# Cross-attention over the cached memory: other buffers and another order for the loads, and two transposes moved ahead of the key transposes

## What is computed

```
def mem_attend(h, mk, mv, wq, wo):
    q = (h @ wq).reshape(bsz, t, M_HEADS, M_HEAD_DIM)          # 4 heads of 256
    s = einsum("bthd,bmhd->bhtm", q, mk) * (M_HEAD_DIM ** -0.5)
    p = softmax(s, axis=-1)
    o = einsum("bhtm,bmhd->bthd", p, mv)
    return o.reshape(bsz, t, M_WIDTH) @ wo

# prompt:  mk, mv are computed from mem_prompt, and are outputs too (mem_k_prompt, mem_v_prompt)
# samples: mk, mv = cache_mem_k[l], cache_mem_v[l], each (8, 256, 4, 256) float32
```

## Time and profile before

| | |
|---|---|
| median of three executions | 2195.84 us |
| the profiled execution, its own time | 2198.57 us |
| its span in the trace | 2196.8 us |
| TensorE busy | 2097.8 us, 95% |
| VectorE busy | 992.3 us, 45% |
| ScalarE busy | 762.1 us, 35% |
| GpSimd busy | 195.9 us, 9% |
| DMA over the whole span | 219.94 MB, 100 GB/s |

### The profile page before, as it was taken

The page is one execution under the profiler, slowest core; times in us unless marked ns, Lnnn a source line. Parts: engine busy times, 40 slices in busy tenths (PEclk is TensorE's granted clock), DMA queues, the critical chain, the costliest instruction groups (busy, mean ns, idle before and its releaser), DMA issues.

```text
span 2196.8 us, 30506 instructions
## 1 busy us (share of the span) xinstructions
PE 2097.8 (95%) x12346; PEld 1850.5 (84%) x12346; DVE 992.3 (45%) x1675; ACT 762.1 (35%) x1314; POOL 195.9 (9%) x454
## 2 busy tenths in 40 slices
PE   7999869999989999999999999999989999999997
PEld 6888649898668999999988888779857999999996
DVE  5453463343534444344444547662553444444443
ACT  3222441243523432323323545333542432233232
POOL 2011111000010000000000114210010000000001
PEclk9999887999999999999999999999999999999999
DMA  6223213124552212222221121442482212222221
GB/s 196 94 92 126 107 58 96 58 87 145 210 195 77 77 58 77 77 87 77 78 91 60 58 77 44 149 152 88 163 317 70 77 58 77 77 87 77 77 77 52
DMA packets 111048, 219.94 MB, mean 100 GB/s; under 512 B 6994, under 2 KB 52350, under 8 KB 110844
## 3 DMA queue, kind: packets, MB, share of 16 engines
q1 hardware_dynamic: 89920, 143.80, 19.7%
q0 software_dynamic: 20416, 72.09, 9.3%
q10 hardware_dynamic: 576, 2.10, 0.2%
HBM read 201.03 MB, written 18.24 MB: 100 GB/s over the span
## 4 chain that ended last, share of the span: by engine, by line
PE 89%; DVE 4%; ACT 3%; DMA 3%; issue 1%; POOL 0%; SPq 0%; ACTq 0%; DVEq 0%; POOLq 0%
PE bank L734 14%; PE bank L736 14%; PE bank L735 14%; PE bank L798 7%; PE bank L794 7%; PE bank L796 7%; PE bank L793 5%; PE bank L795 5%; PE bank L797 5%; DMA kcX<-cache_mem_k 2%; PE bank L1008 1%; PE bank L1097 1%; PE bank L757 1%; PE bank L1075 1%; PE bank L996 1%
## 5 line engine op out<-in xcount | busy, mean ns | idle before, releaser
L1876 DVE TENSOR_TENSOR w_lo<-raw,w_hi 128x1024 fp32r<-128x1024 f32 x265 | 319.1, 1221 | 581.3 <-ACT w_hi L1400 576.9
L1400 ACT ACTIVATE w_hi<-raw 128x1024 fp32r<-128x1024 f32 x265 | 274.1, 1052 | 309.7 <-PE bank L736 254.9
L734 PE MATMUL bank<-w_hi,hT_lo 128*128 128x512 f32 x720 | 287.7, 400 | 3.8 <-DVE w_lo L1876 1.8
L794 PE MATMUL bank<-hT_hi,w_lo 128*128 128x384 f32 (+1 forms) x856 | 289.3, 338 | 0.0
L796 PE MATMUL bank<-hT_lo,w_hi 128*128 128x384 f32 (+1 forms) x856 | 289.3, 338 | 0.0
L798 PE MATMUL bank<-hT_hi,w_hi 128*128 128x384 f32 (+1 forms) x856 | 289.3, 338 | 0.0
L736 PE MATMUL bank<-w_hi,hT_hi 128*128 128x512 f32 x720 | 282.4, 392 | 0.0
L735 PE MATMUL bank<-w_lo,hT_hi 128*128 128x512 f32 x720 | 282.4, 392 | 0.0
L793 PE MATMUL bank<-hT_hi,w_lo 128*128 128x256 f32 (+1 forms) x856 | 239.7, 280 | 0.0
L795 PE MATMUL bank<-hT_lo,w_hi 128*128 128x256 f32 (+1 forms) x856 | 239.0, 279 | 0.0
L797 PE MATMUL bank<-hT_hi,w_hi 128*128 128x256 f32 (+1 forms) x856 | 239.0, 279 | 0.0
(11 more groups left out here) (359 smaller groups left out, 3114.8 us busy)
## 6 DMA issues: line engine op xcount, KB each, us to landing
raw<-w_ffn_gate SPq DMA_DIRECT2D x44, 512.0 KB, 4.0
raw<-w_ffn_up SPq DMA_DIRECT2D x44, 512.0 KB, 5.1
raw<-w_ffn_down SPq DMA_DIRECT2D x22, 1024.0 KB, 4.9
kcX<-cache_mem_k POOLq DMA_DIRECT2D x16, 1024.0 KB, 7.0
vcX<-cache_mem_v POOLq DMA_DIRECT2D x16, 1024.0 KB, 8.7
raw<-w_in_even SPq DMA_DIRECT2D x14, 1024.0 KB, 5.3
raw<-w_in_odd SPq DMA_DIRECT2D x12, 1024.0 KB, 5.1
raw<-w_cq SPq DMA_DIRECT2D x8, 1024.0 KB, 7.2
```

The source lines that it names most:

```text
L734: pe.matmul(out, wl, xh, start=first, stop=False)
L794: pe.matmul(ob, wl, hT_hi[:, k, HA:TOK], start=f, stop=False)
L1400: act.activation(w_hi[:, g % W_SLOTS, 0:n], raw[:, q % 2, UNIT * i:UNIT * i + n], ACT.Copy).then_inc(*hi_made.mark(c, u))
L1876: dve.tensor_tensor(w_lo[:, s, 0:n], raw[:, q % 2, UNIT * i:UNIT * i + n], flat(w_hi[:, s, 0:n]), ALU.subtract).then_inc(*lo_made.mark(c, u))
```

## The change

It has three parts. First, memory: `kcX[1]` moves from 53248 (over `mk`) to 28672 (over `mv`), and `kTX[0]` the other way, from 28672 to 53248. Second, GpSimd's stream: the store `o_mv` is issued right behind `o_mk`; k0 follows when the last prompt scores are made; and k1, which now needs `mv` to be free, waits for `crossP` and for `put["mv"]`. v0 and v1 stand behind k1. ScalarE and VectorE no longer wait for `put["mv"]` in step 0. Third, the order inside a step on TensorE: the transposes of `pS` and `oS` come ahead of the 16 key transposes, and ScalarE copies their results ahead of its two key copies. VectorE's order in a step stays. No instruction is added or taken away but the waits.

```diff
--- before.py
+++ after.py
@@ -351,9 +351,9 @@
         mk = at("mk", 53248, [P, 2, D])
         pX = at("pX", 61440, [P, 2, 2, MEM])
         pXT = at("pXT", 0, [P, TP, H, 2, P])
-        kcX = [at("kcX0", 20480, [P, 2, D]), at("kcX1", 53248, [P, 2, D])]
+        kcX = [at(f"kcX{i}", 20480 + 8192 * i, [P, 2, D]) for i in range(2)]
         vcX = [at(f"vcX{i}", 36864 + 8192 * i, [P, 2, D]) for i in range(2)]
-        kTX = [at("kTX0", 28672, [P, 8, MEM]), at("kTX1", 0, [P, 8, MEM])]
+        kTX = [at("kTX0", 53248, [P, 8, MEM]), at("kTX1", 0, [P, 8, MEM])]
         pS = at("pS", 61440, [P, 2, MEM])
         pST = at("pST", 63488, [P, 2, 2, P])
         oS = at("oS", 65536, [P, 2, MEM])
@@ -597,20 +597,23 @@
                 for m in range(2):
                     pool.wait_ge(*act_done.at("mk", l, m, 1))
                 pool.dma_start(io["o_mk"][l].rearrange("(m p) n -> p m n", p=P), mk[:, :, :]).then_inc(*put["mk"].mark(l))
+                for m in range(2):
+                    pool.wait_ge(*act_done.at("mv", l, m, 1))
+                pool.dma_start(io["o_mv"][l].rearrange("(m p) n -> p m n", p=P), mv[:, :, :]).then_inc(*put["mv"].mark(l))
+
+
                 def mem_kv(cache, b):
                     i = b % 2
                     buf, src = (kcX[i], io["cache_mem_k"]) if cache == "k" else (vcX[i], io["cache_mem_v"])
                     pool.dma_start(buf[:, :, :], src[(l * NB + b) * MEM:(l * NB + b + 1) * MEM, :].rearrange("(m p) n -> p m n", p=P)).then_inc(*loads[f"{cache}x{i}"].mark(l, b))
 
-                pool.wait_ge(*aux_full.at("mkT", l, 1, 1))
+
+                pool.wait_ge(*aux_full.at("sX", l, TP - 1, 1))
                 pool.wait_ge(*put["mk"].at(l))
+                mem_kv("k", 0)
+                pool.wait_ge(*pe_done.at("crossP", l))
+                pool.wait_ge(*put["mv"].at(l))
                 mem_kv("k", 1)
-                for m in range(2):
-                    pool.wait_ge(*act_done.at("mv", l, m, 1))
-                pool.dma_start(io["o_mv"][l].rearrange("(m p) n -> p m n", p=P), mv[:, :, :]).then_inc(*put["mv"].mark(l))
-                pool.wait_ge(*aux_full.at("sX", l, TP - 1, 1))
-                mem_kv("k", 0)
-                pool.wait_ge(*lin_full.at(("cv", l, 1), 1))
                 mem_kv("v", 0)
                 mem_kv("v", 1)
                 for b in range(NB):
@@ -1099,6 +1102,21 @@
                 pe_done.after("crossP", l)
 
                 for s in range(NB + 3):
+                    if 2 <= s < NB + 2:
+                        b = s - 2
+                        pe.wait_ge(*dve_done.at("pS", l, b))
+                        out = lin.open(pe, "pST", l, b)
+                        for m in range(2):
+                            ins = pe.transpose(out[:, P * m:P * m + P], pS[:, b % 2, P * m:P * m + P], ident[:, :])
+                        ins.then_inc(*lin_full.mark("pST", l, b))
+                    if s >= 4 and s % 2 == 0:
+
+                        p = s // 2 - 2
+                        pe.wait_ge(*lin_a.at("oXs", l, p))
+                        out = lin.open(pe, "oXT", l, p)
+                        for j in range(2):
+                            ins = pe.transpose(out[:, P * j:P * j + P], oS[:, p % 2, P * j:P * j + P], ident[:, :])
+                        ins.then_inc(*lin_full.mark("oXT", l, p))
                     if s < NB:
                         pe.wait_ge(*loads[f"kx{s % 2}"].at(l, s))
                         for n in range(4):
@@ -1108,21 +1126,6 @@
                                     k = 2 * n + hd
                                     ins = pe.transpose(out[:, MEM * hd + P * m:MEM * hd + P * m + P], kcX[s % 2][:, m, P * k:P * k + P], ident[:, :])
                             ins.then_inc(*aux_full.mark("kTX", l, s, n))
-                    if 2 <= s < NB + 2:
-                        b = s - 2
-                        pe.wait_ge(*dve_done.at("pS", l, b))
-                        out = lin.open(pe, "pST", l, b)
-                        for m in range(2):
-                            ins = pe.transpose(out[:, P * m:P * m + P], pS[:, b % 2, P * m:P * m + P], ident[:, :])
-                        ins.then_inc(*lin_full.mark("pST", l, b))
-                    if s >= 4 and s % 2 == 0:
-
-                        p = s // 2 - 2
-                        pe.wait_ge(*lin_a.at("oXs", l, p))
-                        out = lin.open(pe, "oXT", l, p)
-                        for j in range(2):
-                            ins = pe.transpose(out[:, P * j:P * j + P], oS[:, p % 2, P * j:P * j + P], ident[:, :])
-                        ins.then_inc(*lin_full.mark("oXT", l, p))
                     if 1 <= s <= NB:
                         b = s - 1
                         pe.wait_ge(*act_done.at("kTX", l, b, 2))
@@ -1634,13 +1637,6 @@
                     act.wait_ge(*lin_full.at("oXp", l, k))
                     act.activation(hT_hi[:, k, 0:SEQ], lin.bank("oXp", l, k)[:, :], ACT.Copy).then_inc(*hT_hi_made.mark("oXp", l, k))
                 for s in range(NB + 3):
-                    if s == 0:
-                        act.wait_ge(*put["mv"].at(l))
-                    if s < NB:
-                        for n in (0, 2):
-                            act.wait_ge(*aux_full.at("kTX", l, s, n))
-                            act.activation(kTX[s % 2][:, 2 * n:2 * n + 2, :], aux.bank("kTX", l, s, n)[:, :].rearrange("p (k m) -> p k m", k=2), ACT.Copy).then_inc(*aux_a.mark("kTX", l, s, n))
-                            act_done.after("kTX", l, s, n)
                     if 2 <= s < NB + 2:
                         b = s - 2
                         act.wait_ge(*lin_full.at("pST", l, b))
@@ -1652,6 +1648,11 @@
                         cols = slice(SEQ + 32 * p, SEQ + 32 * p + 32)
                         act.activation(hT_hi[:, :, cols].rearrange("p (h j) q -> p h j q", j=2), lin.bank("oXT", l, p)[:, 0:2 * P].rearrange("p (j h q) -> p h j q", j=2, h=H),
                                        ACT.Copy).then_inc(*act_done.mark("oX", l, p))
+                    if s < NB:
+                        for n in (0, 2):
+                            act.wait_ge(*aux_full.at("kTX", l, s, n))
+                            act.activation(kTX[s % 2][:, 2 * n:2 * n + 2, :], aux.bank("kTX", l, s, n)[:, :].rearrange("p (k m) -> p k m", k=2), ACT.Copy).then_inc(*aux_a.mark("kTX", l, s, n))
+                            act_done.after("kTX", l, s, n)
                     if 1 <= s <= NB:
                         b = s - 1
                         act.wait_ge(*dve_done.at("negXs", l, b))
@@ -2187,8 +2188,6 @@
                     dve.wait_ge(*hT_hi_made.at("oXp", l, k))
                     dve.tensor_tensor(hT_lo[:, k, 0:SEQ], lin.bank("oXp", l, k)[:, :], flat(hT_hi[:, k, 0:SEQ]), ALU.subtract).then_inc(*lin_v.mark("oXp", l, k))
                 for s in range(NB + 3):
-                    if s == 0:
-                        dve.wait_ge(*put["mv"].at(l))
                     if s < NB:
                         for n in (1, 3):
                             dve.wait_ge(*aux_full.at("kTX", l, s, n))
```

More of the change, by code:

```diff
@@ L1101, in rest @@
                 for s in range(NB + 3):
-                    if s < NB:
-                        pe.wait_ge(*loads[f"kx{s % 2}"].at(l, s))
-                        for n in range(4):
-                            out = aux.open(pe, "kTX", l, s, n)
-                            for hd in range(2):
-                                for m in range(2):
-                                    k = 2 * n + hd
-                                    ins = pe.transpose(out[:, MEM * hd + P * m:MEM * hd + P * m + P], kcX[s % 2][:, m, P * k:P * k + P], ident[:, :])
-                            ins.then_inc(*aux_full.mark("kTX", l, s, n))
                     if 2 <= s < NB + 2:
@@ L1125, in rest @@
                         ins.then_inc(*lin_full.mark("oXT", l, p))
+                    if s < NB:
+                        pe.wait_ge(*loads[f"kx{s % 2}"].at(l, s))
+                        for n in range(4):
+                            out = aux.open(pe, "kTX", l, s, n)
+                            for hd in range(2):
+                                for m in range(2):
+                                    k = 2 * n + hd
+                                    ins = pe.transpose(out[:, MEM * hd + P * m:MEM * hd + P * m + P], kcX[s % 2][:, m, P * k:P * k + P], ident[:, :])
+                            ins.then_inc(*aux_full.mark("kTX", l, s, n))
                     if 1 <= s <= NB:
```

## The result

The changed kernel took 2210.36 us, the median of four executions (2209.39 to 2216.25), against 2194.49 for the kernel before, measured beside it. The ratio is 1.0079, with a 95% interval from 1.0054 to 1.0103: slower by 12 to 23 us. (The two medians alone give 1.0072, 15.9 us, which lies inside it.) All fifteen executions of the changed kernel on record took 2206.50 to 2219.41 us, with a median of 2209.82. The profiled execution took 2207.48 us, with a span of 2205.7.

The account below looks back on a forecast made before the run. The prediction took transfers to bound most of the loop, with room only at its edges. Loads and order, 14.7 us, plus the clock, 3.7, made 18.4 us; against 2195.84 that is 2214.2 us, range 2205 to 2224.

Parts of the forecast that it names:

- rival (1): In the loops, the softmax wait hides and only the loads count: 2205.8 us, or 2209 with the clock; chance 0.14.
- What bounds the loop, and that a delay goes straight into the time: Transfers bind most of the loop; TensorE has 89% of the chain, so its delays go straight into the time.
- Part one, the loads: At the loop's start k1, v0 and v1 are issued later, inside the loop: some 5 us per layer.
- Part two, the order: In each loop step, `pS` ahead of the keys exposes the softmax; a step takes at least 5.33 us in the mean.
- The sum of both parts: Late loads and new order together, in the two loops: 7.5 and 7.2 us, 14.7 us in all.
- Part three, edits at nothing: Dropped `mv` waits, k1 moved from 547 us, swapped addresses, ScalarE's earlier copy: nothing, down to -0.3 us a step.
- Part four, the clock: Step 2's key transposes, behind the longest gap, run at half TensorE clock: 1.85 us in each loop, 3.7 us in all.
- (2): Idle DMA time in the loop takes the three added loads: +1 to +2 us per layer, 2199 us; chance 0.05.
- (3): TensorE's clock stays low through the loop: 21 us per layer more, 2254 us; chance 0.06.
- (4): In the loops, scores and values follow the keys' landing sooner and idle queue time closes: -7 us, 2189 us; chance 0.03.
- (5): The change does nothing, because GpSimd's k1, v0 and v1 came no earlier in truth: no difference; chance 0.01.

Follow-up runs that it names:

- e11: The kernel before, unchanged, run again for a second profile: loops of 46.7 and 45.2 us.
- e1: The changed kernel with the order inside a step taken back on TensorE and ScalarE, so late loads only: ratio 1.0032 to the kernel before.
- e2: The kernel before with `pS` and `oS` ahead of the key transposes on TensorE and ScalarE, its loads kept: ratio 1.0018 to the kernel before.
- e8: The changed kernel with 4 thrown-away matmuls of 512 columns in the gap ahead of step 1's key transposes: ratio 1.0078 to the kernel before.
- e5: The kernel before with key transposes last in each step on TensorE, ScalarE and VectorE, GpSimd's order kept: ratio 1.0024 to the kernel before.
- e10: e5 with v(b) issued ahead of k(b+2) in GpSimd's stream: 2189.40 us against 2195.69 for the kernel before, ratio 0.9967.

## Why the prediction was right

The forecast was 2214.2 us with a range of 2205 to 2224; measured were 2210.36. As a difference, 18.4 us were forecast and 15.9 measured beside the kernel before. The time alone proves little: rival (1) with the clock's part came to 2209. What bears the prediction out is the trace. By its steps:

- *What bounds the loop, and that a delay goes straight into the time.* Right in the main: 14.1 us more in the two loops against the mean of two profiles of before (12.6 and 15.6 against each), 15.9 in the medians. That nothing outside the loops would move by more than 2 us didn't hold for single profiles: 10.5 us less ahead of the first loop and 3.7 more between them, where the kernel before itself moved by 7.7 and 2.8 (e11).
- *Part one, the loads.* Step 1's transposes were expected 5.6 us into the loop, behind a gap of 3.7 us; they began 5.8 us into it (588.45 less 582.69), behind gaps of 3.77 and 3.72. k2 was expected 13.7 us into the loop, it landed at 13.3 (596.0 less 582.69). The loads alone were set at 5 us a loop; e1 has 6.1 by the profile and 3.5 by the whole (7 us for two loops).
- *Part two, the order.* The step was set at 5.33 us in the mean and came out at 5.42: the scores follow each other by 5.31 and 5.52 us in turn in layer 1. The wait for line 2203 was set at 1.1 us and was 1.19. Set at 2.5 us a loop in the sum of both parts; e2 gave 2.3 by the profile and 2 by the whole. Counted from the loop's start, the scores of sequence 7 began at 46.8 and 46.1 us, where 45.7 had been worked out without the clock's part. That all loads of steps 5 to 7 come in time failed narrowly in layer 0: k7 was 0.26 us late.
- *The sum of both parts*, 7.5 and 7.2 us for loops of 52.0 us: measured 52.7 and 51.8.
- *Part three, edits at nothing.* Nothing in the trace speaks against it; it wasn't tried apart.
- *Part four, the clock: mis-sized, in the place.* The clock fell in the first gap, between 587 and 588 us, and came back between 594 and 595, as the stretches below show. But the slow blocks were step 1's, not step 2's. They stand in the chain that ended last, and yet cost next to nothing: they and the softmax behind them were over 0.25 us (layer 0) and 0.15 us (layer 1) after k2 had landed, and without them step 2 would have waited for k2. So where 1.85 us a loop had been put down, some 0.2 were paid, and the gap ahead of step 2 (1.98 us) is put down to line 2203 and not to a `kcX` load, as the prediction had it. That the clock's term is too large by 3.3 us and the forecast too high by 3.8 is near enough, but no proof, with medians of the kernel before that differ by 1.4 us. e8 shows the forecast course when step 1 is kept at full clock.
- *Rivals.* (1), the softmax hidden, is refuted by the chain of the changed kernel, whose waits for line 2203 stand in every step, and by the intervals of e1 and of the changed kernel, which don't meet; (2) by the loops of e1, each over 3 us longer than any of the kernel before; (3), the clock low through the loop, by the 1.95 us of the key transposes from step 2 on; (4) and (5) by the time.

TensorE's clock in the changed kernel, stretches of 1 us (length, PE busy, clock, DMA share, GB/s):

```profile
586.00:587.00 1.00, 0.00 (x0) 1.00 1.02 418
587.00:588.00 1.00, 0.00 (x0) 0.68 1.00 410
588.00:589.00 1.00, 0.55 (x3) 0.50 1.05 434
...
593.00:594.00 1.00, 0.99 (x12) 0.50 1.04 418
594.00:595.00 1.00, 0.00 (x0) 0.91 1.06 426
```

It fell to 1.2 GHz after TensorE had stood since 584.7 us, and rose to 2.4 GHz after a stretch in which it was busy, the transposes being most of that work. By the Trainium skill ("TensorE: Matmul & The Clock Gate", section "Part 4: PE-mode transpose") the full clock isn't granted for transposes. In this trace it came back behind 3.68 us of transposes and 1.93 us of scores. The second profile of the kernel before (e11) has a case with transposes alone, behind a wait of 2.34 us in layer 0; TensorE's block, and the stretches of 1 us:

```profile
614.50 3.52 PE L1109 MATMUL bank<-ident,kcX 128*128 128x128 f32 x16 [2.34 <-DMA kcX<-cache_mem_k]
```

```profile
614.00:615.00 1.00, 0.50 (x3) 0.65 1.01 414
615.00:616.00 1.00, 1.00 (x6) 0.50 1.01 414
...
617.00:618.00 1.00, 1.00 (x8) 0.64 1.04 414
618.00:619.00 1.00, 1.00 (x17) 1.00 1.00 401
```

The clock fell to 1.2 GHz about when the block began. The 0.64 of the microsecond from 617 puts its rise to 2.4 GHz at about 617.7 us, and from 614.50 until the `pS` pair at 617.85 TensorE did nothing but these key transposes. The page's sentence doesn't hold for them.

## What to carry to other kernels

In a loop fed by double-buffered transfers, write down for each step two lengths, that of the queue (here 2 x 2.71 us) and that of the longest chain through the engines (here 5.33 us by the working and 5.42 measured, with the softmax exposed): where they are equal, a reorder that looks free takes away the room in which late loads could be made up. A load that waits for a buffer holds up every load behind it in the same stream, so those whose buffers are free go first; and when the order of a step is changed, the issuing engine's order has to follow it (e5 against e10, 0.24% slower against 0.33% faster). A slow block behind a gap costs next to nothing where a transfer that the next step needs lands at the same time as it ends (changed kernel), and its whole excess where none does (e8); look at which step it falls on before it goes into the sum.

## What was not expected of the hardware

- One matmul of 512 float32 columns appears as two entries 0.43 us apart: 8 of them took 7.03 us (16 entries), 4 took 3.60. The trace of the kernel before had this already: the 32 entries of 14.0 us at line 1097 are 16 matmuls in the kernel, and the 16 entries of a score product are 8. The 16 key transposes are 16 entries.
- Keeping TensorE busy with discarded work moved the slow clock from step 1 to step 2 in both loops of e8 and made them longer (56.2 and 53.5 against 52.7 and 51.8 us, part of it a later v7).
- The same kernel has loops of 44.3 to 46.7 us and a part ahead of them that ends at 585 or 593 us. From 200 us to the first loop TensorE was busy for 351.8 us at a granted clock of 0.93 in the one execution and for 360.6 us at 0.91 in the other; what makes the clock differ isn't shown.
